# The second layer of the first block: another table for the work between the steps of its heads

## The chip, the cores and the metric

The kernel runs on one core of a Trainium2 chip. The metric is the device time of one execution, in microseconds (us). Several runs of a kernel give a median; one further execution is recorded by the hardware profiler, and all rows shown here come from it. The engines are TensorE (PE, matmuls; its weight loads are listed apart as PEld), VectorE (DVE), ScalarE (ACT), GpSimd (POOL) and SyncE (SP, which here issues the transfers of weights from HBM).

## What is computed

Two transformer blocks of two layers each, on 256 tokens of width 1024, in fp32. Only the second layer of the first block matters here. It works on a stream x and a context c:

```python
h  = modulate(rms_norm(x, norm1_g[l]), sh1, sc1)
hc = modulate(rms_norm(xc, norm1_g[l]), csh1, csc1)
q, k, v, up, ca, cb = project_inputs(h, w_in[l], q_norm_g[l], k_norm_g[l])
qc, kc, vc, upc, cac, cbc = project_inputs(hc, w_in[l], q_norm_g[l], k_norm_g[l])
q = apply_rope(q, cos, sin); k = apply_rope(k, cos, sin)
k_all = jnp.concatenate([kc, k], axis=3); v_all = jnp.concatenate([vc, v], axis=2)
attn = diff_attn_post(diff_attention(q, k_all, v_all, lam), subln_g[l], lambda_init)
pool_o = pool_mixer(up, pool_w[l], pool_scale[l])
conv_o = conformer_conv(ca, cb, conv_dw_w[l], conv_dw_b[l], conv_ln_g[l], conv_ln_b[l])
mix = jnp.concatenate([attn, pool_o, conv_o], axis=-1)
x = x + g1 * jnp.einsum('blm,md->bld', mix, w_out[l])
```

`diff_attention` has four heads with two softmaxes each, which are subtracted. `conformer_conv` has a convolution of 31 taps over 256 channels, a layer norm and a silu. sh1, sc1, g1 and their like come from `silu(c) @ w_mod[l]`, a product of width 6144 that the kernel takes in pieces.

## The kernel before

**Weights.** All weights come in pieces of about 1 MB, in one fixed sequence that the planner finds by recording the order of their use. SP issues their transfers into three raw buffers (`raw`, `NRAW`), each when its buffer is free. A projection's piece is then split in two halves into `wh` (ACT, an fp32r copy, line 1762) and `wl` (DVE, the rest, line 2009), of which there are three pairs; PE makes three products, `hi*wh`, `hi*wl` and `lo*wh` (lines 1546, 1549, 1551, or 1564 to 1568 for v). A piece of `w_mod` (2048 columns) is not split: PE reads it from its raw buffer (`mod`, `raw,csil`), and so the buffer is held from the landing to that product.

**Order.** `plan_program` writes one list of steps, and every engine walks that list and takes its own part, in order. An engine that waits for a semaphore holds up everything behind it in its own part. Nothing is reordered at run time.

**The stage.** The second layer's projections come as two generators: `gc` for the context (k0, v0, k1, v1) and `gx` for x (b, a, p, q0, k0, v0, q1, k1, v1). Before this part `gc` has run two of its parts and `gx` six. What is left is k1 and v1 of c and q1, k1, v1 of x. Of the w_mod product eight pieces are left (`m`), then its bias and transpose (`modend`, line 1601 on PE). A q or k projection is followed by `hn1` (ACT squares it and multiplies it by a gain) and `hn2` (PE sums the squares with `tmp,cst`, and swaps pairs for x; ACT takes the root; DVE makes the rope, lines 2064 to 2069). The 62 steps of the convolution (31 taps for each of two channel halves, DVE, line 2002 `pcx<-upadx,vec,pcx`) are given out 10 at a time behind the projections. `conv1` (mean, PE `pcx,cst`), `conv2` (variance) and `conv3` (silu, with an ACT table load before it and one after, line 1753) end it, and `pc_split` writes the pool and convolution half of the mixed vector to `hc_hi` and `hc_lo`.

**Heads.** `attention1` goes through eight units, one for each head and half of the queries. In a unit stand scores (`sc1`, PE `k,q1x`), row maxima and exponentials (`exp1`: DVE line 2110, ACT line 1763), weights (`wt1`: DVE lines 2117, 1998, 2002, writes `e`), and a turn of the 128x512 weights (`turn1`: PE line 1647, ACT copies to `aT`). Each second unit ends with the value product (`val1`, PE `aT,v`), ACT's square of it, and the head's norm (`sub1`: PE sum, ACT root, DVE and ACT write `hc`). The generator yields twelve times. `outproj1` takes four weight pieces: two for the pool and convolution half of the mixed vector, then two for the heads' half.

**The table.** Ahead of each of the heads' twelve steps a string of letters tells what is put in:

```python
for names in IN_SECOND:
    for name in names.split():
        portion[name]()
    next(at, None)
```

K is the next projection of c, P of x, m a piece of w_mod, S settles what is pending (all taps out), x `conv1`, N `conv2`, A `conv3`, Z `pc_split`, O a step of the output product, s and h split the next piece or half a piece ahead of its use, t gives out four taps if any are left. A projection splits pieces ahead by itself when it can. After the strings `weave(out)` runs the rest of the output product, `mod_fill` the rest of the m, and then comes the norm for the feed-forward part.

Of the kernel before, what the change touches and what calls it, by code (L numbers as in the profile page):

```python
# [15 lines left out]
P = 128  # L16
# [147 lines left out]
class Memory:  # L164
    def __init__(self, nc, banks):
# [33 lines left out]
        for i in range(2 * NSPLIT):  # L199
# [73 lines left out]

IN_FIRST = ("m G", "", "G m", "m G", "G", "G h", "m x t", "m", "c m m", "m h", "S m h N s m", "A m m", "m",
            "s m t T h m Z Y t O h h", "h O s m m", "O m", "O m", "", "m", "m")
IN_SECOND = ("K m P m", "P m K m", "P m S x m", "N A m Z m", "O m", "O m", "", "", "", "", "", "")

# [169 lines left out]
def plan_program(M, pieces):  # L449
# [423 lines left out]
    def pc_split(s, dst):  # L873
        assert conv_tok[s][0].sem == "cact" and not pending_pool
        t = (ev("mx_hi"), ev("mx_lo"))
        step("pcsplit", s=s, out=H[dst], ready=flat([conv_tok[s], pool_tok[s]]), free=list(hfree[dst]), t=t)
        pc_free[s] = list(t)
        mix_of[s][4:8] = [t] * 4
# [147 lines left out]
    def finish_conv(l, s):  # L1026
        pump(len(bg))
        two.append(conv_post(l, s))
# [82 lines left out]
    for g in (gc, gx, gx, gx, gx, gx, gx):  # L1111
# [5 lines left out]
                    "x": lambda: finish_conv(1, "x"), "Z": lambda: pc_split("x", "c"), "O": lambda: next(out)})  # L1117
    for names in IN_SECOND:
        for name in names.split():
# [1417 lines left out]
```

How the kernel before makes its waits and increments, by code:

```python
    def wait_ge(self, *events):  # L1514
        for e in flat(events):
            if self.seen.get(e.sem, 0) < e.val:
                self.eng.wait_ge(self.sems[e.sem], e.val)
                self.seen[e.sem] = e.val
# [18 lines left out]
    def gemm(f, nk, ncols, tiles, a, a_toks, k0, first, last, free, t_half, w0, t, **_):  # L1537
        for k in range(nk):
            half = (w0 + k) * ncols >= f["cut"]
            x_hi, x_lo = a[0][:, k0 + k, :], a[1][:, k0 + k, :]
            for j, (c, m, o, b) in enumerate(tiles):
                out = b.t[0:m, o:o + T]
                on.wait_ge(f["thi"][half], a_toks[k0 + k][0])
                if first and k == 0:
                    on.wait_ge(free[j])
                pe.matmul(out, block(f, M.wh, w0 + k, ncols, c, m), x_hi, start=first and k == 0 and o == 0, stop=False,
                          skip_group_check=True)
                on.wait_ge(f["tlo"][half])
                pe.matmul(out, block(f, M.wl, w0 + k, ncols, c, m), x_hi, start=False, stop=False, skip_group_check=True)
                on.wait_ge(a_toks[k0 + k][1])
                ins = pe.matmul(out, block(f, M.wh, w0 + k, ncols, c, m), x_lo, start=False, stop=last and k == nk - 1,
                                skip_group_check=True)
            if t_half and (w0 + k + 1) * ncols == f["cut"]:
                ins.then_inc(*on.inc(t_half))
        ins.then_inc(*on.inc(t))
# [1 line left out]
    def gemm_tok(f, nk, b, free, a, a_toks, t_half, t, **_):  # L1557
        on.wait_ge(free)
        for k in range(nk):
```

## Time and profile before

| | us |
|---|---|
| median of 3 runs | 1672.39 (1670.56 to 1675.26) |
| profiled execution, its own time | 1672.15 |
| its span, first to last instruction | 1670.3 |
| PE busy in the span | 1607.1 |
| mean granted TensorE clock | 0.99 of full |

The span is what the trace covers; the 1.9 us around it are the rest of the execution. Stretches and rows are given in us from the start of the span. PE's records overlap where matmuls are pipelined, so the time between two starts, not the length of a row, is what one costs in a row of them. "idle" in brackets is the time in which the engine did nothing ahead of a row, with what ended it. A mean granted clock of 1.00 is 2.4 GHz, 0.50 is 1.2 GHz. Idle time of an engine costs something only where the end waits for it; on PE, which is full nearly everywhere, it does.

### The profile page before, as it was taken

What the parts mean: (1) busy time and instruction counts of PE and PEld (TensorE: products, weight loads), DVE (VectorE), ACT (ScalarE), POOL (GpSimd) and SP (SyncE); (2) the same over time, 40 slices, a digit from 0 to 9 for tenths busy, and PEclk for the clock granted to TensorE, in tenths of its full rate; (3) what the DMA queues carried; (4) which work ended last, traced back from release to release, by engine and by line L of the source; (5) the groups of instructions that cost most, each with busy time, mean ns of one, the idle gap of its engine ahead of it and who ended that gap; (6) DMA issues with size and microseconds to landing.
All of it is one profiled execution on the core that took longest, in us unless ns stands there. A gap on an engine that the chain in (4) does not pass through costs nothing. (4 is left out here: it accounts for less than half of the span.)

```text
span 1670.3 us, 31133 instructions
## 1 busy us (share of the span) xinstructions
PE 1607.1 (96%) x12918; PEld 1476.0 (88%) x12918; DVE 1112.2 (67%) x1736; ACT 922.6 (55%) x1467; POOL 156.7 (9%) x136
## 2 busy tenths in 40 slices
PE   5999999999999999998899999998999999999999
PEld 3987479999999999965799999878999998789999
DVE  2799667645566655887664456777887567778873
ACT  3444756545464444546454446766665467666662
POOL 1230000111001110300011100000011000001010
PEclk8999999999999999998999999999999999999999
DMA  9443765666546554464366554213555642235553
GB/s 382 166 152 127 262 243 204 254 228 218 192 176 214 188 191 172 152 243 163 107 197 203 191 187 166 94 55 125 202 190 189 225 142 91 77 128 204 195 192 123
DMA packets 45164, 301.09 MB, mean 180 GB/s; under 512 B 5232, under 2 KB 7504, under 8 KB 11744
## 3 DMA queue, kind: packets, MB, share of 16 engines
q1 hardware_dynamic: 44304, 297.44, 50.2%
q8 instruction: 102, 1.67, 0.4%
q0 software_dynamic: 288, 0.92, 0.1%
q10 hardware_dynamic: 432, 0.75, 0.1%
q14 instruction: 38, 0.31, 0.1%
HBM read 298.02 MB, written 1.06 MB: 179 GB/s over the span
## 5 line engine op out<-in xcount | busy, mean ns | idle before, releaser
L2009 DVE TENSOR_TENSOR wl<-raw,wh 128x1040 fp32r<-128x1040 f32 (+1 forms) x472 | 569.8, 1245 | 319.0 <-ACT wh L1762 225.0
L1762 ACT ACTIVATE wh<-raw 128x1040 fp32r<-128x1040 f32 (+1 forms) x472 | 465.4, 1031 | 180.5 <-PE bank L1551 94.7
L1546 PE MATMUL bank<-hx_hi,wh 128*128 128x256 f32 x1856 | 523.2, 282 | 7.3 <-ACT hx_hi L1762 7.3
L1551 PE MATMUL bank<-hx_lo,wh 128*128 128x256 f32 x1856 | 516.4, 278 | 0.0
L1549 PE MATMUL bank<-hx_hi,wl 128*128 128x256 f32 x1856 | 515.3, 278 | 0.1
L1546 PEld LDWEIGHTS bank<-hx_hi,wh 128*128 128x128 f32 x1856 | 349.8, 188 | 13.7 <-issue 12.8
L1549 PEld LDWEIGHTS bank<-hx_hi,wl 128*128 128x128 f32 x1856 | 349.8, 188 | 4.3 <-issue 3.8
L1551 PEld LDWEIGHTS bank<-hx_lo,wh 128*128 128x128 f32 x1856 | 349.7, 188 | 0.7 <-DVE hx_lo L2002 0.4
L1546 PE MATMUL bank<-hid_hi,wh 128*128 128x256 f32 x912 | 252.7, 277 | 1.4 <-ACT hid_hi L1762 1.3
L1549 PE MATMUL bank<-hid_hi,wl 128*128 128x256 f32 x912 | 252.2, 277 | 0.9 <-DVE wl L2009 0.9
L1551 PE MATMUL bank<-hid_lo,wh 128*128 128x256 f32 x912 | 252.2, 276 | 0.2
L1546 PE MATMUL bank<-hc_hi,wh 128*128 128x256 f32 x784 | 223.5, 285 | 8.1 <-issue 7.6
L1551 PE MATMUL bank<-hc_lo,wh 128*128 128x256 f32 x784 | 220.0, 281 | 2.2 <-DVE hc_lo L2138 1.2
L1549 PE MATMUL bank<-hc_hi,wl 128*128 128x256 f32 x784 | 219.4, 280 | 0.1
L1546 PEld LDWEIGHTS bank<-hid_hi,wh 128*128 128x128 f32 x912 | 171.3, 188 | 2.1 <-ACT hid_hi L1762 1.7
L1549 PEld LDWEIGHTS bank<-hid_hi,wl 128*128 128x128 f32 x912 | 171.3, 188 | 1.4 <-DVE wl L2009 1.3
L1551 PEld LDWEIGHTS bank<-hid_lo,wh 128*128 128x128 f32 x912 | 171.2, 188 | 0.6 <-DVE hid_lo L2002 0.6
L1546 PEld LDWEIGHTS bank<-hc_hi,wh 128*128 128x128 f32 x784 | 149.2, 190 | 18.9 <-issue 16.1
L1551 PEld LDWEIGHTS bank<-hc_lo,wh 128*128 128x128 f32 x784 | 149.0, 190 | 3.1 <-DVE hc_lo L2138 1.4
L1549 PEld LDWEIGHTS bank<-hc_hi,wl 128*128 128x128 f32 x784 | 149.1, 190 | 0.9 <-DVE wl L2009 0.4
L1762 ACT ACTIVATE tmp<-bank,vec 128x256 f32<-128x256 f32 (+3 forms) x180 | 100.0, 582 | 43.5 <-PE bank L1574 39.3
L1762 ACT ACTIVATE tmp<-bank 128x512 f32<-128x512 f32 (+4 forms) x102 | 57.0, 562 | 118.8 <-PE bank L1551 91.1
(220 smaller groups left out, 1936.8 us busy)
## 6 DMA issues: line engine op xcount, KB each, us to landing
raw<-in_wts SPq DMA_DIRECT2D x208, 1032.0 KB, 4.9
raw<-in_wts SPq DMA_DIRECT2D x50, 1024.0 KB, 6.7
raw<-in_wts SPq DMA_DIRECT2D x20, 776.0 KB, 4.2
raw<-in_wts SPq DMA_DIRECT2D x4, 584.0 KB, 4.6
tmp<-tscr SPq DMA_DIRECT2D x16, 128.0 KB, 3.9
raw<-in_wts SPq DMA_DIRECT2D x2, 648.0 KB, 3.9
xTc<-in_ctxT SPq DMA_DIRECT2D x1, 1024.0 KB, 10.8
xTx<-in_xT SPq DMA_DIRECT2D x1, 1024.0 KB, 7.2
```

The costliest lines, as they stand in the source:

```text
L1546: pe.matmul(out, block(f, M.wh, w0 + k, ncols, c, m), x_hi, start=first and k == 0 and o == 0, stop=False, skip_group_check=True)
L1549: pe.matmul(out, block(f, M.wl, w0 + k, ncols, c, m), x_hi, start=False, stop=False, skip_group_check=True)
L1551: ins = pe.matmul(out, block(f, M.wh, w0 + k, ncols, c, m), x_lo, start=False, stop=last and k == nk - 1, skip_group_check=True)
L1762: return act.activation(out, in_, func, bias=bias, scale=scale)
L2009: tt(M.wl[k][:, cols], M.raw[r][:, cols], M.wh[k][:, cols].bitcast(F32), ALU.subtract).then_inc(*on.inc(lo))
```

## The change

One line. The strings of `IN_SECOND` are others:

```diff
@@ -273,7 +273,7 @@
-IN_SECOND = ("K m P m", "P m K m", "P m S x m", "N A m Z m", "O m", "O m", "", "", "", "", "", "")
+IN_SECOND = ("K P s s", "m P", "K S m", "x", "N h m h A m", "Z P s s", "m h m", "", "t O m", "", "m O", "")
```

The last two of the ten `m` of the old table find no piece left. The old table puts the two remaining projections of c and the three of x ahead of the first three steps of the heads; the new one spreads them over the first six, the w_mod pieces over eleven, conv's three steps over the fourth and fifth, and the two O behind the eighth and the tenth. Each engine has the same work in both.

On PE, behind the context's v1 projection (`wh_58,hc_lo` ends it; `raw` is a w_mod piece, `cst,e` a turn, `k_90,q1x` scores, `pcx,cst` conv's mean, `aT_98,v_91` a value product; two scores are one unit):

```order
 L1568 MATMUL bank<-wh_58,hc_lo 128x256
+L1574 MATMUL bank<-raw_55,csil 32x512 x4
+L1647 MATMUL bank<-cst,e_0_94 128x128 x4
+L1574 MATMUL bank<-k_90,q1x 128x512 x2
+L1574 MATMUL bank<-pcx,cst 128x256 x2
+L1647 MATMUL bank<-cst,e_1_96 128x128 x4
+L1574 MATMUL bank<-k_90,q1x 128x512 x2
+L1574 MATMUL bank<-tmp_86,cst 128x256 x2
+L1574 MATMUL bank<-raw_56,csil 32x512 x4
 L1574 MATMUL bank<-raw_57,csil 32x512 x4
-L1574 MATMUL bank<-k_90,q1x 128x512 x4
+L1574 MATMUL bank<-aT_98,v_91 128x256 x4
```

Before, a w_mod piece and the scores of units 1 and 2 stood here ahead of x's v1 projection; now two units' turns, conv's mean and variance and head 0's value product stand ahead of it.

On DVE, between the rope of x's first k piece and the maxima of unit 0 (`st_60`; `pcx` are taps, `wl` the lower halves of split weights):

```order
-L2002 SCALAR_TENSOR_TENSOR pcx<-upadx,vec,pcx 128x256 x18
+L2002 SCALAR_TENSOR_TENSOR pcx<-upadx,vec,pcx 128x256 x8
+L2009 TENSOR_TENSOR wl_71<-raw_56,wh_70 128x1040
+L2009 TENSOR_TENSOR wl_71<-raw_56,wh_70 128x1024
+L2002 SCALAR_TENSOR_TENSOR pcx<-upadx,vec,pcx 128x256 x10
 L2059 TENSOR_TENSOR k_90<-tmp_82,tmp_83 128x2x256
-L2009 TENSOR_TENSOR wl_71<-raw_57,wh_70 128x1040
-L2009 TENSOR_TENSOR wl_71<-raw_57,wh_70 128x1024
+L2009 TENSOR_TENSOR wl_61<-raw_57,wh_58 128x1040
+L2009 TENSOR_TENSOR wl_61<-raw_57,wh_58 128x1024
 L2002 SCALAR_TENSOR_TENSOR pcx<-upadx,vec,pcx 128x256 x10
 L2110 TENSOR_REDUCE st_60<-bank 128x1 x2
```

One more split (of the context's v1 weights) stands ahead of unit 0's maxima now; it was behind them.

On ACT, around conv's silu (`pcx<-pcx,vec`). Before, with the split of the first output piece and `pc_split` behind it:

```order
L1762 ACTIVATE tmp_84<-tmp_84 128x256
L1762 ACT_TABLE_LOAD
L1762 ACTIVATE pcx<-pcx,vec 128x256 x2
L1753 ACT_TABLE_LOAD
L1762 ACTIVATE wh_70<-raw_57 128x1040
L1762 ACTIVATE wh_70<-raw_57 128x1024
L1762 ACTIVATE hc_hi<-pcx 128x1024
```

And now, with the split of x's v1 weights ahead and head 0's square, turn and exponentials behind:

```order
L1762 ACTIVATE tmp_84<-tmp_84 128x256
L1762 ACTIVATE wh_64<-raw_55 128x1040
L1762 ACTIVATE wh_64<-raw_55 128x1024
L1762 ACT_TABLE_LOAD
L1762 ACTIVATE pcx<-pcx,vec 128x256 x2
L1753 ACT_TABLE_LOAD
L1762 ACTIVATE tmp_87<-bank 128x256
L1762 ACTIVATE aT_98<-bank 128x4x128
```

So `pc_split` and the first output product, which came next, now come behind head 0's norm and behind x's v1 projection.

## Rows read from the trace of the kernel before

**Rows 1.** Page, busy us; then stretches: length, PE, PEld, DVE, ACT, POOL busy, PEclk.

```profile
PE 1607.1 (96%) x12918; PEld 1476.0 (88%) x12918; DVE 1112.2 (67%) x1736; ACT 922.6 (55%) x1467; POOL 156.7 (9%) x136
...
600.00:700.00 100.00, 100.00 (x848) 98.16 (x848) 64.44 (x77) 51.35 (x66) 17.68 (x15) 1.00 0.53 185
700.00:800.00 100.00, 87.11 (x537) 63.81 (x536) 75.50 (x149) 52.24 (x96) 0.00 (x0) 0.93 0.47 169
```

**Rows 2.** The same view, of the stretch that the change reorders.

```profile
702.00:799.50 97.50, 84.61 (x528) 62.20 (x528) 73.50 (x144) 50.89 (x94) 0.00 (x0) 0.93 0.48 174
```

**Rows 3.** Waits of PE, 702 to 817: us in total, times, longest.

```profile
PE bank L1546 <- issue: 4.4, 1, 4.4
PE bank L1574 <- ACT tmp L1762: 4.2, 3, 2.5
PE bank L1574 <- ACT aT L1762: 3.5, 3, 1.7
```

**Rows 4.** Busy time by stretches: the three at half clock (PEclk is third from last).

```profile
757.60:764.40 6.80, 4.94 (x21) 4.68 (x22) 5.67 (x11) 4.53 (x9) 0.00 (x0) 0.50 0.56 200
788.30:791.70 3.40, 3.40 (x12) 2.52 (x10) 3.16 (x10) 1.83 (x5) 0.00 (x0) 0.50 0.00 0
795.20:798.60 3.40, 3.40 (x8) 2.22 (x7) 0.00 (x0) 0.00 (x0) 0.00 (x0) 0.51 0.00 0
```

**Rows 5.** PE in order of time: start us, us, what, count [idle before, releaser].

```profile
707.82 1.06 PE L1574 MATMUL bank<-raw,csil 128*32 128x512 f32 x8
...
728.47 1.98 PE L1574 MATMUL bank<-tmp,cst 128*128 128x512 f32 x4 [2.54 <-ACT tmp L1762]
...
758.55 0.55 PE L1546 MATMUL bank<-hc_hi,wh 128*128 128x256 f32 x1 [4.42 <-issue]
...
795.03 3.65 PE L1574 MATMUL bank<-aT,v 128*128 128x256 f32 x8 [1.67 <-ACT aT L1762]
...
813.06 1.99 PE L1574 MATMUL bank<-tmp,cst 128*128 128x256 f32 x8 [1.14 <-ACT tmp L1762]
```

**Rows 6.** PE in order of time: what the steps take at full clock.

```profile
717.46 1.98 PE L1574 MATMUL bank<-tmp,cst 128*128 128x512 f32 x4
...
724.86 1.06 PE L1574 MATMUL bank<-raw,csil 128*32 128x512 f32 x8
...
747.85 0.66 PE L1647 MATMUL bank<-cst,e 128*128 128x128 f32 x4
...
767.55 0.60 PE L1601 MATMUL bank<-cst,tmp 128*128 128x128 f32 x4
...
779.86 1.99 PE L1574 MATMUL bank<-aT,v 128*128 128x256 f32 x8
```

**Rows 7.** ACT in order of time: unit 0's exponential, conv's silu, the split behind.

```profile
723.34 0.69 ACT L1763 ACTIVATE e<-bank,st 128x512 f32<-128x512 f32 x1 [6.44 <-DVE st L1998]
...
751.79 1.28 ACT L1762 ACT_TABLE_LOAD   x1
...
754.19 1.28 ACT L1753 ACT_TABLE_LOAD   x1
...
757.41 1.04 ACT L1762 ACTIVATE hc_hi<-pcx 128x1024 fp32r<-128x1024 f32 x1
```

**Rows 8.** Waits of SP's queue; ACT's split at 713.82; transfers, median us to landing.

```profile
SPq L2343 <- PE bank L1574: 49.5, 8, 15.0
...
713.82 2.02 ACT L1762 ACTIVATE wh<-raw 128x1040 fp32r<-128x1040 f32 x2 [2.48 <-DMA raw<-in_wts]
...
raw<-in_wts SPq DMA_DIRECT2D x6, 1024.0 KB, 6.0
```

**Rows 9.** DVE in order of time: taps, a split, a unit's maxima.

```profile
707.75 7.22 DVE L2002 SCALAR_TENSOR_TENSOR pcx<-upadx,vec,pcx 128x256 f32<-128x256 f32 x18
...
715.48 2.38 DVE L2009 TENSOR_TENSOR wl<-raw,wh 128x1040 fp32r<-128x1040 f32 x2
...
739.87 1.28 DVE L2110 TENSOR_REDUCE st<-bank 128x1 f32<-128x512 f32 x2
```

## The prediction

> **What bounds the kernel now.** I read the page's first lines, then the busy time by stretches. TensorE (PE) is busy 1607.1 of 1670.3 us, and the stretch before this layer's input stage is full: 600 to 700 us shows 100.00 of 100. From 700 to 800 us PE is busy 87.11, at a mean granted clock of 0.93 [rows 1]. There the change acts. Both programs do the same work between the projection of the context's second k piece (from 702) and the output products over the heads (from 799.5): 97.5 us with 84.61 busy [rows 2], so 12.9 us of waits. The list of PE's waits from 702 to 817 says for what: 4.4 under "issue", 4.2 for ACT's tmp (1.14 of it behind 799.5), 3.5 for ACT's aT, the rest small [rows 3, 5]. The reader is to see that no single wait bounds it: each is a step of a head with nothing of another kind beside it.
>
> The 4.42 us ahead of 758.55 are typed "issue". They end 0.1 us after ACT's hc_hi<-pcx (757.41 and 1.04 long) [rows 5, 7]: the convolution's output, behind two table loads and a weight split on ACT.
>
> The second loss is the clock. Three stretches stand at half clock (0.50, 1.2 GHz), with 4.94, 3.40 and 3.40 us of PE work in them [rows 4]; the same work at 2.4 GHz takes half, so they lose 5.9 us. The first follows the 4.42 us wait, the others the turns and value products of the last heads, where PE waits 1.67 us ahead of a value product that then reads 3.65 us long against 1.99 at full clock [rows 5, 6]. So the stretch is 78.7 us of work at full clock, 12.9 of waits, 5.9 of clock.
>
> **What the change moves.** No engine gets other work; the same instructions stand in another order. A unit is one head and one half of the queries; there are eight, with scores, exponentials, weights and a turn each, and a value product and a norm sum per head. (a) The eight modulation pieces stand all ahead of unit 1's turn before; now four of them come behind head 0's value product. (b) The scores of units 0 to 2 stand ahead of the context's v1 projection, not those of unit 0 alone. (c) The x stream's v1 projection (6.0 us) goes from ahead of conv's mean to between units 2 and 3, and the two output products over the pool and conv half (5.8 us each) from behind units 1 and 2 to behind unit 5 and behind unit 7. (d) Weight splits are made earlier, as the piece queue no longer holds a modulation piece in a buffer while PE projects: before, SP waits up to 15.0 us for PE to release such a piece, and ACT then 2.48 us for weights to land [rows 8].
>
> **Laying the new order out.** I lay the changed order's instructions end to end on each engine, with the durations of the rows, and note where PE must wait. DVE sets the pace first: from 707.75 to 739.87 it hardly stands idle before. Its 18 taps in 7.22 us (0.40 each), a lo split of 2.38 (2.3 to the next start) and two row maxima of 1.28 (1.4 with the scaling) are rows [rows 9]; a rope is four operations of the same 128x512, 2.65 from first to last start, and a unit's weights 1.7. On PE, from start to start: a projection with its norm sums 7.4 (717.46 to 724.86), a projection alone 6.0, a modulation piece 1.0, a turn 0.6, a value product 1.8 [rows 5, 6]; a pair of scores or a conv sum 1.05 and a head's norm sum 0.5, which are two to four of the matmuls of these rows.
>
> 1. The context's k1 projection ends at 707.82. The modulation piece that filled ACT's squaring (0.6 and its hand-over) is gone: PE waits **0.8**.
> 2. DVE: 8 taps to 710.9, split 713.2, 10 taps 717.2, 0.6, split 720.05, 10 taps 724.0, maxima of unit 0 to 725.4, against 723.1 before. ACT stands in order behind these maxima, as it does now with 6.44 us [rows 7]. Its two exponentials free the banks of unit 2's scores at 726.1 and 726.8. PE is there at 725.75: waits **0.6**. ACT then makes a root (1.3) and has squared x's k1 at 728.75; PE's norm sum waits **1.3** (before, 2.54 at the same place [rows 5]).
> 3. PE projects the context's v1 to 736.4, then a modulation piece, a turn, scores: 739.0. The taps end on DVE at 740.2 (before 739.87; one split of 2.3 less ahead of it, one unit's maxima and weights more, and 0.9 of waiting less). Conv's mean waits **1.3**. Unit 1's weights are behind unit 2's maxima, 743.3: its turn waits **2.0**.
> 4. PE to 751.6: turn, scores, conv's variance, two modulation pieces, head 0's values, turn, scores. ACT: exponentials of unit 3 to 746.8, conv's root 747.75, a split of 2.0, table load 1.28, conv's silu 1.1, table load 1.28 [rows 7], and only then head 0's square at 753.8. PE waits **2.2**, then 0.1 for the bank of the next projection. This chain was behind the 4.42 us wait; now the 6.0 us v1 projection stands between it and its next reader, the output product, so that wait is gone.
> 5. From 754.4 PE: projection (to 760.45), turn, scores, two pieces, values, turn, scores, norm sum (768.1), turn, output product (774.8), piece, values, turn, norm sum, turn, piece, output product (786.5), values, norm sum. ACT and DVE have slack in the 6 us blocks. I find waits of **0.3** (unit 5's turn), **0.5** (unit 7's, behind a split on DVE) and **0.5** (head 3's norm sum).
>
> Waits: 0.8+0.6+1.3+1.3+2.0+2.2+0.1+0.3+0.5+0.5 = 9.6. The transpose of the modulation vector (L1601, 0.4 [rows 6]) goes behind the output products, where PE waits 1.14 for squares anyway [rows 5]: 0.4 less here and nothing there; without that cover it would cost the 0.4. The 3.3 us from 813.06 to the next layer half stay as they are.
>
> DMA: the x stream's v1 piece is requested only at 737.3, behind a modulation product, and split at 748, so the cover of its landing (6.0 us in the median for the modulation's pieces, which are as large [rows 8]) is 5 us. The last two pieces before the output products over the heads are requested at about 776 and 781 and read at 789 and 795.
>
> **The clock** has no wait of 4 us left to follow. But from 739 to 754 there are 5.5 us of waits in 15 us, and PE's work is turns and scores, like the stretch from 779 to 799 that has two half-clock stretches. The bounds are 0 and the 5.9 us of before; I take one short stretch, 1.7 us, as the nearest row has it (3.40 at half clock), since waits of 2.0 and 2.2 are nearer to the 1.67 that preceded one than to none.
>
> **The sum.** Gain = (12.9 - 9.6) + (5.9 - 1.7) + 0.4 = 7.9 us. The profiled execution takes 1672.15 with its span of 1670.3, 0.2 under the median 1672.39 of three (1670.56 to 1675.26). So 1672.4 - 7.9 = 1664.5 us.
>
> **Waits bounded.** Laid out by hand, a wait can be off by a hand-over (about 0.1) or by an ACT step that comes in order. The lower end, 5 us, is if ACT's and DVE's chains of steps 2 to 4 are each 1.5 us shorter than laid; the upper, 12 us, if head 0's chain and a landing cost another 2.4. With the clock's ends the gain is 14.2 (1658.2) or 1.3 (1671.1).
>
> **A page against a row.** The two table loads read 1.28 us each [rows 7]. The Trainium skill ("ScalarE: Activation LUTs", section "Table sets: the hidden batching unit") gives about 2.7 us for a load and says to batch by set. By its price step 4's wait would be 5.0 and the time 1667.3. The trace disagrees with the figure, so the sum goes by the row.
>
> **Rivals.**
> - *The order keeps the clock and the light stretch runs tighter.* For it: both half-clock stretches of the last heads vanish surely, as 6 us projections stand between the units. Waits 7, clock 0: gain 12.2, 1660.2 us. Chance 0.2.
> - *The waits only move.* DVE's taps end at 740 either way, and everything behind them (conv, unit 1's weights, conv's silu) is as late as it was; light work and waits gather at 739 to 754, and half clock comes there twice or more, 4.5 us. Waits 11.5: gain 1.4+1.4+0.4 = 3.2, 1669.2 us. Against it: ahead of unit 0's weights DVE now has no rope and no split of 2.3 [rows 9] between its maxima and them, so the first heads run some 5 us earlier even if the taps do not. Chance 0.2, and it is no change that can be told.
> - *Slower: half clock through the whole light stretch.* If PE's clock falls to 1.2 GHz at 744 and does not rise before the first output product at 768, the 21 us of work in between take twice as long; some 3 us of waits hide in it. That is 18 us against the 9.6 that the order gives without any loss of clock: 8.4 us slower, 1680.8. It decides from 9.6 us of full-clock work done at half clock; the longest stretch in [rows 4] holds 4.94 us, which is 2.5 at full clock, and the unbroken 6 us projection at 754.4 speaks against it too. Chance 0.04.
> - *The change moves nothing that matters*, since weights land late at three more places, by 2.48 us each as at 713.82 [rows 8]: 7.4 of the 7.9 us go, 1671.9 us. Against: every request but one is earlier relative to its reader. Chance 0.04.
>
> The forecast has 0.52. About 0.3% (5.0 us) is what a measurement of this kernel can tell from no change, so faster means under 1667.4. The forecast's case lies there but for a tenth of it; with the first rival faster is 0.2 + 0.52 and a little of the second rival less that tenth, 0.70; same 0.25; slower 0.05. The range of 8 in 10 takes in both of the first rivals, and stops short of the ends 1658.2 and 1671.1: 1658.5 to 1670.
>
> **What would show it.** In the profile after: PE's waits in the stretch sum to some 9 to 10 us, none over 3; the 4.42 us one gone; the longest ahead of head 0's norm sum (L1574, ACT tmp) and unit 1's turn (L1647); DVE's last taps at 740; no half-clock stretch between 754 and 790; the first product over the heads at 789 to 792. Wrong would be: a wait for DMA on PE or ACT of over 2 us, half clock there after all, or waits that sum to over 12.

## The result

| | before | changed |
|---|---|---|
| median, us | 1672.39 (1669.96 to 1675.26, 5 runs) | 1662.38 (1660.61 to 1664.26, 5 runs) |
| span of the profiled execution | 1670.3 | 1660.6 |
| mean granted TensorE clock | 0.991 | 0.991 |

The ratio is 0.9938, with a 95% interval of 0.9927 to 0.995: the change makes the kernel 10 us faster (0.6%). In a second set of runs, below, it was 1662.56 against 1671.74, ratio 0.9944 (0.9932 to 0.9957).

The changed kernel's busy time: the page's line (busy, share, instructions), and stretches (length, PE, PEld, DVE, ACT, POOL busy, PEclk). They answer to [rows 1, 2, 4].

```profile
PE 1604.4 (97%) x12918; PEld 1475.6 (89%) x12918; DVE 1111.6 (67%) x1736; ACT 922.1 (56%) x1467; POOL 156.8 (9%) x136
...
704.04:791.77 87.73, 79.04 (x525) 58.85 (x523) 72.68 (x140) 50.32 (x94) 0.00 (x0) 0.98 0.47 174
757.40:760.80 3.40, 3.40 (x19) 3.40 (x18) 1.25 (x3) 2.82 (x7) 0.00 (x0) 0.50 0.43 180
```

The stage begins 2.0 us later in this trace than in that of before, so both are taken from the same matmul to the same matmul: from the pool's product in the stream ahead to the first output product over the heads. Before, that is

```profile
702.03:799.50 97.47, 84.58 (x528) 62.20 (x527) 73.47 (x144) 50.86 (x94) 0.00 (x0) 0.93 0.48 174
```

So it went from 97.47 to 87.73 us: 9.7 us. PE's waits (length less busy) went from 12.9 to 8.7. PE work at half clock went from 11.74 us (a loss of 5.9) to 3.40 (1.7).

That the spans differ by the same 9.7 us is partly chance. Ahead of the stage, where both programs are the same, the changed one's execution had lost 2.0 us (its half-clock stretches at 17, 30 and 211 us are 6.8 us each; before, the first and the last were 3.4). Behind the stage it won 1.9 back, mostly as a half-clock stretch is missing that the trace of before has:

```profile
819.00:822.40 3.40, 3.40 (x18) 3.40 (x17) 3.34 (x9) 2.27 (x6) 0.00 (x0) 0.51 0.11 28
```

Another execution of the old table (`k1_before_short`, below) lacks it too, so it is not put down to the change. Among all traces here the stage begins at 702.0 to 704.9 us, whatever the table; the variants are therefore compared by the stretch as well as by the median.

PE's waits in the changed kernel, in order of time (start, length, what, and in brackets the idle time ahead and what ended it). They answer to [rows 5].

```profile
710.59 1.12 PE L1574 MATMUL bank<-tmp,cst 128*128 128x512 f32 x2 [0.69 <-ACT tmp L1762]
...
728.42 1.79 PE L1574 MATMUL bank<-k,q1x 64*128 64x512 f32 x4 [0.69 <-ACT e L1763]
730.81 1.98 PE L1574 MATMUL bank<-tmp,cst 128*128 128x512 f32 x4 [0.60 <-ACT tmp L1762]
...
742.40 0.45 PE L1574 MATMUL bank<-pcx,cst 128*128 128x256 f32 x1 [1.31 <-DVE pcx L2002]
...
745.38 0.33 PE L1647 MATMUL bank<-cst,e 128*128 128x128 f32 x1 [1.89 <-DVE e L2002]
...
755.83 0.70 PE L1574 MATMUL bank<-tmp,cst 128*128 128x256 f32 x2 [2.37 <-ACT tmp L1762]
...
781.86 0.33 PE L1647 MATMUL bank<-cst,e 128*128 128x128 f32 x1 [0.63 <-DVE e L2002]
...
791.42 0.70 PE L1574 MATMUL bank<-tmp,cst 128*128 128x256 f32 x2 [0.47 <-ACT tmp L1762]
```

These eight are all that the trace shows between rows. The reader is to see that the 4.42 us wait has no successor, that the waits gather at 742 to 756, and that behind it stand only 0.63 and 0.47 up to the heads' output product.

The longest has its reason on ACT, in order of time:

```profile
748.85 0.47 ACT L1762 ACTIVATE tmp<-bank,vec 128x256 f32<-128x256 f32 x1
749.35 0.42 ACT L1762 ACTIVATE tmp<-tmp 128x256 f32<-128x256 f32 x1
749.67 2.00 ACT L1762 ACTIVATE wh<-raw 128x1040 fp32r<-128x1040 f32 x2
751.69 1.28 ACT L1762 ACT_TABLE_LOAD   x1
752.99 1.09 ACT L1762 ACTIVATE pcx<-pcx,vec 128x256 f32<-128x256 f32 x2
754.10 1.28 ACT L1753 ACT_TABLE_LOAD   x1
755.39 0.38 ACT L1762 ACTIVATE tmp<-bank 128x256 f32<-128x256 f32 x1
```

Root, weight split, load, silu, load, and only then head 0's square (0.38), with no idle time between. PE takes its sum 0.06 us after the square.

### The profile page after: what moved, and what is told of

It is laid out like the page before. It is cut to its first block and busy times, and to the rows that moved or that the text cites. A ratio compares the mean times of both kernels' runs of the same rounds, so it can differ in the third digit from the quotient of the medians.

```text
span 1660.6 us, 31134 instructions
## 1 busy us (share of the span) xinstructions
PE 1604.4 (97%) x12918; PEld 1475.6 (89%) x12918; DVE 1111.6 (67%) x1736; ACT 922.1 (56%) x1467; POOL 156.8 (9%) x136
```

## The experiments

All times are medians beside runs of the kernel before on the same chip, whose medians were 1671.7 to 1672.6 us.

### One part of the change alone: the two O late

```diff
-IN_SECOND = ("K m P m", "P m K m", "P m S x m", "N A m Z m", "O m", "O m", "", "", "", "", "", "")
+IN_SECOND = ("K m P m", "P m K m", "P m S x m", "N A m Z m", "", "", "", "", "O", "", "O", "")
```

> The old table with one part of the change alone: the two O (output products over the pool and convolution half) stand behind the eighth and the tenth string instead of the fifth and sixth. Projections, w_mod pieces and conv's steps stay where they were. Theory A (the gain is the sum of many steps, and a light stretch needs blocks of 6 us between its units): the 4.42 us wait ahead of 758.55 goes, and the half clock of the last heads with it, but units 3 to 5 now follow each other on TensorE without a block, at VectorE's pace of some 3.5 us for a unit of 1.6 us on TensorE; 3 to 6 us of new waits at 755 to 770 and half clock there: 1666 to 1671 us, gain 1 to 6. Rival B (the gain is one wait, the output product behind conv's silu, with the half clock behind it, and the half clock of the last heads): gain 4.4 + 2.5 + 2 or more, 1661 to 1664 us, no slower than the whole change.

Measured: 1670.61 us, ratio 0.9988 (0.9977 to 0.9998), a gain of 2. The 4.42 us wait is gone; a longer one has come ahead of head 0's value product, with half clock behind it. PE, then ACT ahead of it:

```profile
760.45 2.08 PE L1574 MATMUL bank<-aT,v 128*128 128x256 f32 x4 [5.35 <-ACT aT L1762]
```

```profile
752.76 1.28 ACT L1762 ACT_TABLE_LOAD   x1
754.06 1.09 ACT L1762 ACTIVATE pcx<-pcx,vec 128x256 f32<-128x256 f32 x2
755.17 1.28 ACT L1753 ACT_TABLE_LOAD   x1
756.46 2.02 ACT L1762 ACTIVATE wh<-raw 128x1040 fp32r<-128x1040 f32 x2
758.38 1.04 ACT L1762 ACTIVATE hc_hi<-pcx 128x1024 fp32r<-128x1024 f32 x1
759.33 0.57 ACT L1762 ACTIVATE tmp<-bank 128x512 f32<-128x512 f32 x1
759.81 0.58 ACT L1762 ACTIVATE aT<-bank 128x512 f32<-128x512 f32 x1
```

Rival B falls: taking away the reader of that chain only shows its next reader. The stretch loses 14.5 us to waits here (95.79 long, 81.28 busy), against 12.9 before, and less to the clock (10.2 us at half clock in place of 13.6, by length). Theory A's range holds the time, close to its upper end.

### The new table with the two O early

```diff
-"Z P s s", "m h m", "", "t O m", "", "m O", "")
+"Z P s s","O","O m h m","t","m","","")
```

> The new table with the two O put back early, behind the sixth and seventh string (one later than in the old table, since no bank is free before), and the w_mod pieces behind them moved up with them; the last three heads' steps have no block between them again. Theory A: the waits up to 754 stay as in the changed kernel (0.7, 0.7, 0.6, 1.3, 1.9, 2.4), and the last heads get back their waits (1.2, 0.3, 1.7, 0.5) and two stretches of half clock (3.4 us lost): 3 to 6 us above the changed kernel, 1665 to 1669 us. Rival C (the gain comes from the projections spread over the first heads, the places of the O do not matter once they stand behind conv's silu): within 1 us of the changed kernel, 1661.5 to 1663.5 us.

The w_mod pieces and half splits move up with them. Measured: 1680.66 us, ratio 1.0055 (1.0041 to 1.0069): 18 us behind the changed kernel and 8 behind the old one. Neither theory had that. In front of head 0's norm sum PE waits 6.70 us, not 2.4, and ACT's rows say why:

```profile
754.00 1.07 ACT L1762 ACTIVATE wh<-raw 128x1040 fp32r<-128x1040 f32 x1 [2.94 <-DMA raw<-in_wts]
755.08 1.28 ACT L1762 ACT_TABLE_LOAD   x1
...
758.78 1.06 ACT L1762 ACTIVATE wh<-raw 128x1024 fp32r<-128x1024 f32 x1
```

```profile
760.16 1.22 PE L1574 MATMUL bank<-tmp,cst 128*128 128x256 f32 x2 [6.70 <-ACT tmp L1762]
```

The place of an O also sets the place of its weights in the one sequence of pieces. They now come right behind x's v1 weights, are requested when a w_mod piece has been read, and are split, in ACT's order, directly behind that request. ACT stands there until they land, and silu, loads and head 0's square stand behind it. Between 702 and 817 ACT waits 12.6 us for weights in two places, 9.6 us in the longer.

### The same with one w_mod piece ahead of each O

```diff
-"N h m h A m", "Z P s s", "m h m", "", "t O m", "", "m O", "")
+"N m m A","Z P","m O","m O","m","m","","")
```

> The new table with the two O a unit or two earlier (seventh and eighth string instead of ninth and eleventh), each behind one w_mod piece, so that the first O's weights are still split where the changed kernel splits them, and conv's steps with no split of an output piece between them. The earlier run of this kind had the split of an output piece on ScalarE ahead of its landing (2.9 and 9.6 us of ScalarE waiting for weights), which this one is meant to be rid of for the first piece. Theory A (blocks of 6 us are wanted between the last heads): the first wait of more than 2.5 us that differs from the changed kernel's is in the last heads, waits of 4 to 7 us more behind 778 and one or two half-clock stretches: 1667 to 1671 us. Rival C (O's place does not matter, the slow result was the split ahead of its landing alone): 1662 to 1664 us. Rival F (the second O's weights and the heads' weights again land late, since they are requested when a w_mod piece is released and split in ScalarE's order at once): waits of ScalarE for raw of 2 us and more at two or three places, 1666 to 1672 us; the trace tells it from A by what ScalarE stands at when TensorE waits.

Measured: 1675.67 us, ratio 1.0022 (1.0011 to 1.0033). Head 0's wait is 2.38 as in the changed kernel. Then ACT stands at two splits, and PE behind the second:

```profile
771.40 1.07 ACT L1762 ACTIVATE wh<-raw 128x1040 fp32r<-128x1040 f32 x1 [4.37 <-DMA raw<-in_wts]
...
788.54 1.07 ACT L1762 ACTIVATE wh<-raw 128x1040 fp32r<-128x1040 f32 x1 [8.48 <-DMA raw<-in_wts]
```

```profile
791.10 0.48 PE L1574 MATMUL bank<-aT,v 128*128 128x256 f32 x1 [3.33 <-ACT aT L1762]
```

This is rival F's sign, but the time is above its range (1666 to 1672) and above theory A's. How much of the 13 us over the changed kernel it makes, the short loads below tell.

### The new table with the w_mod pieces early

```diff
-"K P s s", "m P", "K S m", "x", "N h m h A m", "Z P s s", "m h m", "", "t O m", "", "m O", "")
+"K m P m","m P m","K S m m","x","N A m","Z P","m","","t O","","O","")
```

> The new table with the w_mod pieces put early, six of the eight ahead of unit 0's turn as in the old one, the rest by the eighth string; all else in its place. Theory A (w_mod pieces are the filler of the light stretch and hold raw buffers while TensorE projects): the 0.7 us wait ahead of the context's norm sum goes, but two pieces (2 us) are missing at 748 and two at 765, so waits of 2 to 4 us more at unit 1's turn, head 0's and head 1's norm sum; ScalarE waits for weights again as before the change (2.5 us once or twice): 1664.5 to 1668 us. Rival G (the w_mod pieces' places carry nothing; what counts is where the projections and the O stand): within 1.5 us of the changed kernel.

Measured: 1671.10 us, ratio 0.9994 (0.9986 to 1.0003): the whole gain is gone. ACT waits 6.42 us for weights ahead of 719.61 and again ahead of 747.31, where DVE's lower split, the row maxima and unit 1's weights stand behind it:

```profile
747.31 2.02 ACT L1762 ACTIVATE wh<-raw 128x1040 fp32r<-128x1040 f32 x2 [3.89 <-DMA raw<-in_wts]
```

```profile
753.95 1.12 PE L1647 MATMUL bank<-cst,e 128*128 128x128 f32 x4 [6.75 <-DVE e L2002]
```

Rival G falls. Theory A's range (1664.5 to 1668) is missed as well: it had ACT's waits for weights at 2.5 us.

### Short loads: late weights apart from the order

Four kernels load 24 pieces of the stage in an eighth of their columns, so that no split is long late (a load of a piece takes 2.1 us in the median here, against 6.0 with all columns). All engines do the same instructions, on old values in the other columns, so the output is another:

```diff
-        sp.dma_start(M.raw[r][:, 0:ne], io["wts"][row, :, 0:ne]).then_inc(*on.inc(t, 16))
+        n = 256 if 88 <= row <= 111 else ne
+        sp.dma_start(M.raw[r][:, 0:n], io["wts"][row, :, 0:n]).then_inc(*on.inc(t, 16))
```

> The kernel before, with the 24 weight pieces of this stage (the last seven w_mod pieces, q, k, v and the output product's) loaded in an eighth of their columns only (256 of 2048), so that they land in about 2 us instead of 5 to 6; TensorE, VectorE and ScalarE do all their work, on stale values in the rest. Theory A (the wait for the output product is ScalarE's order, not the landing): the 4.4 us ahead of the first output product stays within 1 us, ScalarE's 2.48 us for weights at 714 goes: 1669.5 to 1672.5 us. Rival F (late weights are what the old order loses by): 4 us or more faster, under 1668.5 us.

> The changed kernel with the same short loads. Theory A: in the changed kernel ScalarE waits for weights once, 1.7 to 2.4 us at 788, and TensorE nowhere: 1661 to 1663 us, so that the change gains 8 to 10 us here as well. Rival F (a part of the gain is that weights land in time): its lead on the old table with short loads shrinks to 6 us or less.

> The new table with the two O a unit or two earlier, which came out at 1675.7 us with full loads, ScalarE standing 4.4 and 8.5 us at the split of weights that had not landed. With short loads these go. Theory A (without a block between the last heads' units TensorE waits for VectorE and ScalarE there): still 3 to 6 us above the changed kernel with short loads, 1665 to 1668 us. Rival F (the loss was late weights alone): within 1.5 us of it, 1661 to 1664 us.

> The new table with the w_mod pieces early, which came out at 1671.1 us with full loads (ScalarE standing 6.4 and 3.9 us at splits, and behind one of them TensorE 6.75 us at unit 1's turn). With short loads, theory A (the pieces are also the filler at 748 and 765): 2 to 4 us above the changed kernel with short loads, 1664 to 1666.5 us. Rival F (their place costs only through the raw buffer and the landing): within 1.5 us of it, 1661 to 1664 us.

| table | full loads | short loads | of the loss, late weights |
|---|---|---|---|
| before | 1671.78 | 1674.17 | |
| changed | 1662.56 | 1661.81 | |
| O a unit early | 1675.67 | 1667.03 | 13.1 less 5.2: 7.9 |
| w_mod early | 1671.10 | 1665.48 | 8.5 less 3.7: 4.8 |

The last column takes differences of differences; each median difference is good to some 2 us only. The stretches bear it out: with short loads that of O a unit early falls from 97.95 to 88.8 us, that of w_mod early from 95.9 to 90.0.

The old table is not faster with short loads (ratio 1.0009, 1.0 to 1.0018), and its stretch is as long as with full ones; that of the changed table is 0.5 us shorter. The stretches of old and new with short loads (columns as above, DMA share second from last):

```profile
702.64:800.13 97.49, 84.64 (x528) 62.19 (x527) 73.43 (x144) 50.72 (x94) 0.00 (x0) 0.93 0.08 22
```

```profile
702.24:789.46 87.22, 79.32 (x524) 57.76 (x523) 72.84 (x140) 50.36 (x94) 0.00 (x0) 0.98 0.08 24
```

The old table's median is above theory A's range; as its stretch is the same, the 2 us are elsewhere and stay open. The lead of the changed table is 12.4 us with short loads, not less than the 9 to 10 with full ones. So the gain is not that weights land in time: it is the order of the work, as theory A has it. The neighbours of the new table lose the larger part of what they lose to late weights. With these out of the way they keep 7.1 us (O early) and 8.7 us (w_mod early) of the 12.4.

For O a unit early, theory A's number came true (5.2 us) and its mechanism did not. The stretch up to the heads' product is 88.8 us, only 1.6 longer than with the changed table. The rest stands behind it, in the norm for the feed-forward part, where PE waits for ACT's last squares. PE, then DVE there:

```profile
808.48 0.80 PE L1574 MATMUL bank<-tmp,cst 128*128 128x256 f32 x1 [2.99 <-ACT tmp L1762]
```

```profile
795.97 4.66 DVE L2009 TENSOR_TENSOR wl<-raw,wh 128x1040 fp32r<-128x1040 f32 x4 [0.54 <-ACT wh L1762]
800.55 1.65 DVE L2002 SCALAR_TENSOR_TENSOR xTx<-bank,modT,xTx 128x256 f32<-128x256 f32 x4
```

In the changed table with short loads DVE has, at the same place,

```profile
792.81 2.38 DVE L2009 TENSOR_TENSOR wl<-raw,wh 128x1040 fp32r<-128x1040 f32 x2 [0.55 <-ACT wh L1762]
795.11 1.68 DVE L2002 SCALAR_TENSOR_TENSOR xTx<-bank,modT,xTx 128x256 f32<-128x256 f32 x4
```

With the O early, two pieces are split between head 3's norm and the first residual sum, in the changed table one; the sum begins 7.9 us after the heads' product has begun, not 5.7, and the 2.3 us go through to the norm (PE waits 2.99, not 0.69). PE then runs at half clock from 807.8 to 818.0. The order of splits has moved with the O, and is paid for some 30 us later. The stretch at half clock:

```profile
807.80:818.00 10.20, 7.40 (x24) 6.17 (x25) 5.66 (x18) 4.98 (x10) 0.00 (x0) 0.50 0.30 104
```

The same table with full loads has it as well (818.8 to 829.0, behind a wait of 3.00), so it is no accident of one execution. The two traces lie unluckily for a sum, though: that of this run took 1668.79 us, the slowest of its six, that of the changed table 1660.68, the fastest of its five. For the w_mod pieces theory A is right in kind: ACT's long waits for weights are gone, 4.33 us remain ahead of unit 1's turn (in place of 1.89) and its stretch is 90.0 us, 2.7 longer.

### Conv's silu behind head 0's norm

```diff
-"N h m h A m", "Z P s s",
+"N h m h m","A Z P s s",
```

> The changed kernel with A (conv's silu with its two table loads on ScalarE) moved from the fifth string to the head of the sixth, behind head 0's value product and norm. Theory D (the 2.37 us wait of TensorE ahead of head 0's norm sum at 755.8 is ScalarE's square standing behind load, silu, load): the wait falls to 0 to 0.3 us, pc_split comes some 2 us later, which the v1 projection covers; if the half clock at 757.4 to 760.8 follows the waits of 741 to 756, it goes too. 1660.0 us with the half clock, 1658.3 without. Rival E (the wait is head 0's own chain: value product, square, copy; or unit 2's turn and the exponentials that now come ahead): the wait stays over 1.5 us or comes back at the next turn, 1662 us.

Measured: 1664.34 us, ratio 0.9951 (0.9938 to 0.9964), within noise of the changed kernel's 0.9938 (0.9927 to 0.995); at least it is not the 1658 to 1660 us of theory D. The 2.37 us wait is gone, so its cause was right: ACT squares at 751.62 and the sum follows the scores at 753.01 without a wait. But a wait comes back ahead of head 1's value product, now behind ACT's load, silu, load, pc_split and split:

```profile
764.63 1.87 PE L1574 MATMUL bank<-aT,v 128*128 128x256 f32 x4 [1.92 <-ACT aT L1762]
```

```profile
756.95 1.28 ACT L1762 ACT_TABLE_LOAD   x1
758.24 1.09 ACT L1762 ACTIVATE pcx<-pcx,vec 128x256 f32<-128x256 f32 x2
759.36 1.28 ACT L1753 ACT_TABLE_LOAD   x1
760.65 1.06 ACT L1762 ACTIVATE hc_hi<-pcx 128x1024 fp32r<-128x1024 f32 x1
761.61 2.00 ACT L1762 ACTIVATE wh<-raw 128x1040 fp32r<-128x1040 f32 x2
763.52 0.58 ACT L1762 ACTIVATE v<-bank 128x512 f32<-128x512 f32 x1
764.00 0.59 ACT L1762 ACTIVATE aT<-bank 128x512 f32<-128x512 f32 x1
```

That is rival E's second form, the wait that comes back at a later reader. The stretch is 89.61 us, 1.9 longer: two half-clock stretches of 3.4 us instead of one, at 744 and at 765.

### Conv's silu left out

```diff
-            fn(y, y, ACT.Silu, scale=M.vcol(("clng", l), j), bias=M.vcol(("clnb", l), j)).then_inc(*on.inc(t_x[j]))
+            fn(y, y, ACT.Identity if l == 1 else ACT.Silu, scale=M.vcol(("clng", l), j), bias=M.vcol(("clnb", l), j)).then_inc(*on.inc(t_x[j]))
```

> The changed kernel, with the convolution's silu in this layer left out: ScalarE scales and adds only, so both table loads (1.28 us each) and nothing else go from its order; the output is another. Theory D: ScalarE is 2.56 us earlier at head 0's square, the wait of 2.37 us ahead of its norm sum falls to 0 to 0.2: 1660.0 us, or 1658.3 if the half clock behind it goes too. Rival E: as in the run before this one, the wait stays and the time is 1662. If a load cost 2.7 us where the trace shows 1.28 us (the Trainium skill, page on ScalarE: Activation LUTs, section on table sets), 5.4 us would go from ScalarE here; the two readings do not differ in TensorE's wait, only in the distance on ScalarE from the split before the loads to the square behind them, which the trace gives.

Measured: 1660.54 us, ratio 0.9932 (0.992 to 0.9945), 3.8 under the variant above. The 1.8 us under the changed kernel are within noise, as the two intervals overlap. ACT's rows:

```profile
749.20 2.00 ACT L1762 ACTIVATE wh<-raw 128x1040 fp32r<-128x1040 f32 x2
...
752.30 0.38 ACT L1762 ACTIVATE tmp<-bank 128x256 f32<-128x256 f32 x1
```

The square begins 3.10 us after the start of the split ahead of it, in the changed kernel 5.72 (749.67 to 755.39): 2.62 us for two loads, 1.31 each. So the trace's 1.28 us is about what a load costs here; the 2.7 us a load of the Trainium skill ("ScalarE: Activation LUTs", "Table sets: the hidden batching unit") is not borne out. The wait of 2.37 is gone; of the 2.6 us, 1.3 are kept (stretch 86.42 against 87.73), and a wait of 0.61 has come at unit 4's turn.

### And pc_split later still

```diff
-"N h m h m","A Z P s s","m h m",
+"N m m","A P","m m Z",
```

> The run with conv's silu behind head 0's norm, and in addition pc_split (ScalarE 1.04 us, VectorE 1.2 us) behind unit 5's exponentials instead of ahead of x's v1 projection. In that run the wait of 2.37 us ahead of head 0's norm sum had gone, and one of 1.92 us had come ahead of head 1's value product, whose aT copy stood behind load, silu, load, pc_split and a split on ScalarE. Theory H (between 747 and 764 ScalarE has no idle time, and TensorE waits for what comes last there wherever it stands): the 1.92 us wait falls by pc_split's 1.0 to 0.9 or less, and if the half clock behind it goes, 1.7 more: 1660.5 to 1663 us. Rival E (it is head 1's own chain): it stays 1.9 us, 1664 us.

Measured: 1666.29 us, ratio 0.9967 (0.9955 to 0.9978), 3.7 behind the changed kernel beside it. Theory H names the wait rightly (1.92 fell to 0.77) and the time wrongly, as two others grew:

```profile
764.50 0.48 PE L1574 MATMUL bank<-aT,v 128*128 128x256 f32 x1 [0.77 <-ACT aT L1762]
...
768.09 0.33 PE L1647 MATMUL bank<-cst,e 128*128 128x128 f32 x1 [1.60 <-DVE e L2002]
...
773.36 0.47 PE L1647 MATMUL bank<-cst,e 128*128 128x128 f32 x1 [2.92 <-DVE e L2002]
```

DVE's lower part of pc_split (1.22 us, at 769.04, 1.01 of idle time ahead of it) now stands between the weights of unit 4 and the maxima of unit 5.

### The changed kernel once more

> The changed kernel once more, on the chip of the runs beside it, as their yardstick. By the ledger of waits its stretch from the context's second k projection to the products over the heads is the same as in the first trace of it: waits 0.7, 0.7, 0.6, 1.3, 1.9, 2.4, 0.6, 0.5, in sum 8.6. Half clock: if a stretch follows from the waits ahead of it, one of 3.4 us stands again at 757; if its place is only loosely tied to them, it stands at 744 to 748 (behind the waits of 1.3 and 1.9), as in the two variants of the new table that were run, or there are two. 1661 to 1663.5 us.

Measured: 1662.56 us (the profiled execution 1664.24). Waits 7.7 in a stretch of 88.0 us: 1.31 and 1.89 as in the first trace, head 0's only 1.54, since PE came later to it: it was at half clock ahead.

```profile
745.00:751.80 6.80, 5.58 (x16) 2.60 (x20) 4.69 (x11) 4.08 (x11) 0.00 (x0) 0.50 0.00 1
```

So the same program has one stretch of 3.4 us at 757 in one execution and one of 6.8 at 745 in another. In the first it begins behind all the waits of 742 to 756, in the second between the first two of them; where it falls is not fixed. The stretch is only 0.3 us longer: 1.1 more is lost to the clock and 1.0 less to waits.

## Why the prediction was right

It forecast 1664.5 us (a gain of 7.9) in a range of 1658.5 to 1670, and 1662.4 (10.0) came. That median stands midway between the forecast and the first rival (1660.2: waits 7, no half clock); what decides is the trace, with 8.65 of waits and a half-clock stretch in every profiled execution of this table. The stretch's ledger:

| step | forecast | profile after |
|---|---|---|
| 1, the context's norm sum | 0.8 | 0.69 |
| 2, unit 2's bank | 0.6 | 0.69 |
| 2, x's norm sum | 1.3 | 0.60 |
| 3, conv's mean | 1.3 | 1.31 |
| 3, unit 1's turn | 2.0 | 1.89 |
| 4, head 0's norm sum | 2.2 + 0.1 | 2.37 |
| 5, units 5 and 7, head 3's sum | 0.3, 0.5, 0.5 | none, 0.63, 0.47 |
| sum of waits | 9.6 | 8.65 |
| half clock | 1.7 | 1.7 (2.8 in the second trace) |

**The laying out** was exact where two engines meet. Taking 2.0 us off for the later begin, DVE's taps ended at 740.3 (forecast 740.2), unit 1's weights at 743.3 (743.3), head 0's square at 753.8 (753.8). The one term that differs much is x's norm sum, 1.3 against 0.60: PE spent 0.66 us of it inside unit 2's scores (1.79 long against 1.13), waiting for the second bank (its second pair starts at 729.09, as ACT's second exponential ends at 729.03), which I had put down as a hand-over. Bank and norm sum together are 1.95, forecast 1.9.

**The gain by terms.** Waits 4.2 (forecast 3.3), clock 4.2 (4.2), the transpose 0.4 (0.4; it went into a place where PE waits 0.70 anyway). That makes 8.8 of 9.7. A part of the missing 0.9 are waits that stand inside rows and count as busy there. Before, two units' scores read 1.88 us (below) and 1.79 (at 782.98) against 1.13 for the others; in the changed kernel one does (1.79 at 728.42).

```profile
777.92 1.88 PE L1574 MATMUL bank<-k,q1x 64*128 64x512 f32 x4
```

That is 1.4 us against 0.7, which my ledger of waits had left out on both sides. The rest, some 0.2, stays open.

**The clock.** The amount was right, the place wrong: I had one short stretch at 739 to 754 and none from 754 to 790. It began at 757.4 (755.4 by the old kernel's times) inside the unbroken projection, 1.6 us after the last wait. The second trace has it at 745 and twice as long, 2.8 us lost. So 1.7 to the tenth is luck, taken from one row between bounds of 0 and 5.9. What I held against the slow rival, that such a projection ends half clock, is too strong; it can begin in one, too.

**"The first heads run earlier"** is what decided against the rival that the waits only move. Some 5 us were forecast; PE's turn of unit 0 begins at 739.37, before at 747.85, which is 10.5 us earlier from the common start, though the taps end as late as before.

**The reason (d)** was wrong as a reason for gain. I credited the freed raw buffer with earlier splits. With short loads the gain is no smaller, so (d) gives nothing. Nor do the letters s and h of the new table do anything: without them the planner, which splits ahead by itself, writes the very same program. Late weights, which I gave 0.04, do not hold PE up here: ACT waits 2.39 us for weights at 788, while PE is in the second output product. They are what its neighbours fail by, though.

**Two of my three signs of being wrong came**, though the time held: a wait for DMA on ACT of over 2 us (these 2.39), and a half-clock stretch between 754 and 790. The first was badly chosen, as it asked how long ACT stands and not whether PE then waits for it; the second is the clock's wrong place. The third, waits over 12, did not come. A side remark was misread: the 3.3 us from 813.06 to the next layer half are 4.16 in the row, and did stay (4.12); no sum used them.

**No single part.** O late alone gives 2 us; from the new table, O early loses 13 to 18 and w_mod early 8.5. Much of these losses is late weights: with short loads they are 5.2 and 3.7 of a gain of 12.4. So the places of the O and of the w_mod pieces carry a part each, and what is left stands with the projections and conv's steps spread over the heads. No run moves those alone; that they carry the rest is not shown. That moving a step can make weights late, and so cost more than the step's place is worth, was not in the prediction, which added terms. None of the variants with the same output is faster than the changed kernel.

## What to carry to other kernels

Lay the new order out on every engine from the rows, wait by wait, and ask at each removed wait who reads the same chain next: the 4.42 us went where a 6 us block stood ahead of the next reader, and came back as 5.35 where there was none. Where weights are prefetched in order of use, a table of steps is a schedule of transfers as well, and a split that an engine meets in order before it has landed stops everything behind it. To tell the two apart, shorten the transfers and leave the order alone.

## What was not expected

- A step moved by a unit or two brought 2.3 us more of waiting and a half-clock stretch of 10.2 us, some 30 us later and in another part of the program, through the order of the weight splits (O a unit early, with short and with full loads).
- The place and length of the half-clock stretch change between executions of one program (3.4 us at 757, 6.8 at 745), while the stretch between the same matmuls stays within 0.3 us.
- Two table loads cost 2.6 us of ACT's time and 1.3 us of PE's stretch.
